# The first products of the RWKV solve ahead of the SSD's norm: a move on one NeuronCore

## The chip, the core and the metric

The program runs on one core of one Trainium2 chip. Its time is the device time in microseconds (us) of one execution, and the number that counts is the median of several runs. The core's engines run side by side, each works through its own list in order, and they wait for each other through semaphores: PE (TensorE, matrix products into PSUM banks), DVE (VectorE), ACT (ScalarE), POOL (GpSimd) and SP (SyncE, which only issues the weights' DMAs here). PE's clock has two levels, 1.2 and 2.4 GHz; the profile shows which was granted.

## What is computed, cut to what matters

Two transformer blocks follow each other on 256 tokens of width 1024. The first block mixes with an SSD (a chunked state-space mixer) and with RWKV-7, side by side:

```python
y = _ssd_chunked(xh, dt, A, Bm, Cm) + d_skip[:, None] * xh        # SSD, two chunks of 128 tokens
y = y.reshape(b, T, SSD_D) * silu(z)                              # gated
y = y.reshape(b, T, SSD_GROUPS, SSD_D // SSD_GROUPS)
y = y * rsqrt(mean(y * y, axis=-1, keepdims=True) + NORM_EPS)     # norm over each of two groups
y_ssd = y.reshape(b, T, SSD_D) * norm_g
...
def step(S, inp):                                                 # RWKV-7, one token
    r_t, w_t, k_t, v_t, a_t, b_t = inp
    sa = einsum("bhij,bhj->bhi", S, a_t)
    S = S * w_t[:, :, None, :] + sa[..., None] * b_t[:, :, None, :] + v_t[..., None] * k_t[:, :, None, :]
    return S, einsum("bhij,bhj->bhi", S, r_t)
...
mix = concatenate([y_ssd, y_rwkv], axis=-1) @ w_out               # then norm, feed-forward, second block
```

The second block attends to a memory of 256 rows; its keys, `rms_norm(mem) @ w_xk_2`, depend on nothing of the first block.

## The kernel before

**Layout.** Everything is held with the feature on the 128 partitions. Weights come in chunks through a ring of four slots (`ring`), loaded by SP in one fixed order; SP waits until the chunk four places earlier has been used. Intermediate values lie in one large tile, `arena`, by hand-written addresses; PSUM's eight banks are `banks[0]` to `banks[7]`. Nothing is scheduled by a planner: each engine's list is the order in which the functions are called at the file's end, and `mark` and `at` give a step a name and a semaphore value to wait for.

**The stretch in question** lies between the SSD and the first chunk of the RWKV solve.

- `pe_ssd` ends with the products of the SSD's outputs ("ssd y", L1010 and L1013). DVE (`dve_ssd`) adds the skip (L1086) and multiplies with the gate (L1090, "ssd gated"), then takes the reciprocal of the memory norm's root (L569, "mem rstd").
- The SSD's norm has these pieces. ACT squares the gated values (L1121); PE sums them over the partitions into columns of bank 0 (`pe_ssd_norm`, L1140); ACT takes the root (L1124); DVE the reciprocal of 4 columns (L1095, "ssd group rates"); PE spreads it over a bank (`pe_ssd_rates`, L1149, "ssd rates bank"); DVE writes the four normed tiles (L1098, "mix1" 0 to 3). Between them `column_rstd` (L576) turns the memory norm's rate into a column.
- The solve inverts a triangular matrix per head and chunk of 128 tokens, eight heads as two sets `g` of four. For each chunk `c`, `products` (L1514) and `base_products` (L1526) make the matrix L in banks 0 and 3 and its 32-wide blocks in banks 1 and 4; DVE masks them into `LT` and `X` (L1711 to L1719) and transposes `X` to `XT` (L1722). Then four levels follow, blocks of 2, 4, 8 and 16 doubling. In each PE makes "P bank" (L1573) from `LT` and `X`, DVE masks it to `P` (L1730), PE makes "dX bank" (L1584) from `XT` and `P`, and DVE adds it to `X` and transposes again (L1737, L1740). PE cannot go on without DVE, so `fill(n)` puts other products between: parts of the memory keys (`pe_mem_part`, L1252, 12 products of 128x256 in f16; two parts make a quarter of the weights' columns), the sums of RWKV's bonus (L1868) and of its gate (L1877), or products that only keep the clock (L1537).
- For the memory keys ACT writes the high half of each quarter of the weights (`mem_high`, L1224) and DVE the low half (`mem_low`, L1231); part 2n waits for `mem_low` n.
- POOL multiplies `R` and `KP` for the bonus (L1903, 128x1024) and clears two buffers of each set (L1842, L1843).

**What sets the order.** The level buffers of the solve (`solve_set`) lie from `SOLVE` on, where the SSD keeps `rawx`, `xbc`, `EX`, `MT` and `zs`; the two sets are 3584 columns each, all laid out alike. So PE, before chunk 0, waits for `mix1` 3 (L1098), the last reader of the SSD's place and of bank 1. POOL's L1903 and the clearing wait for `mix1` 3 too.

Of the kernel before, what the change touches and what calls it, by code (L numbers as in the profile page):

```python
# [23 lines left out]
P = 128  # L24
# [273 lines left out]
def build(nc, w, out, known):  # L298

    with ExitStack() as ctx:  # L300
# [85 lines left out]
        def solve_set(i):  # L386

            a = SOLVE + 3584 * i
            return dict(LT=view(a, 4, C), X=view(a + 512, 4, BASE), XT=view(a + 640, 4, BASE),
                        P=[view(a + 768, 4, BASE // 2), view(a + 832, 4, BASE // 2)], P32=view(a + 896, 4, BASE),  # L390
                        XT128=view(a + 1024, 4, C), X64=view(a + 1536, 4, 64), RK=view(a + 1792, 4, C),
                        ARB=view(a + 2304, 4, C), G=view(a + 2816, 4, 64), U=view(a + 3072, 4, 64))
# [624 lines left out]
        def dve_ssd(dve):  # L1017
# [63 lines left out]

            for g in range(2):
                dve.wait_ge(*at("ssd y", 1, g))
                for j in range(2):
                    i = 2 * g + j
                    nc.vector.scalar_tensor_tensor(YS[:, i, :], XS(i), par("ssd_d", i), halves(5 + g)[:, j, :],  # L1086
                                                   ALU.mult, ALU.add).then_inc(*mark("ssd_vector"))
                dve.wait_ge(*so_far("ssd_vector"))
                dve.wait_ge(*at("z silu", g))
                nc.vector.tensor_tensor(YS[:, 2 * g:2 * g + 2, :], YS[:, 2 * g:2 * g + 2, :],  # L1090
                                        zs[:, 2 * g:2 * g + 2, :], ALU.mult).then_inc(
                    *mark("ssd_vector", "ssd gated", g))
            norm_reciprocal(dve, "mem")
            dve.wait_ge(*at("ssd group root"))
            nc.vector.reciprocal(group_rate, group_rate).then_inc(*mark("ssd_vector", "ssd group rates"))  # L1095
            dve.wait_ge(*at("ssd rates bank"))
            for i in range(4):
                nc.vector.scalar_tensor_tensor(mix[:, i, :], YS[:, i, :], par("ssd_norm", i), halves(1)[:, i // 2, :],  # L1098
                                               ALU.mult, ALU.mult).then_inc(*mark("ssd_vector", "mix1", i))

        def act_ssd(act):
# [22 lines left out]
            nc.scalar.activation(group_rate, banks[0][:, 0:4], ACT.Sqrt, bias=eps[:, 0:1],  # L1124
# [9 lines left out]
        def pe_ssd_norm(pe):  # L1134
            for g in range(2):
                pe.wait_ge(*at("ssd squares", g))
                pe.wait_ge(*at("ssd exponent", 0, 1, 3))
                for c in range(NC_):
                    for j in range(2):
                        mm = nc.tensor.matmul(banks[0][:, 2 * g + c:2 * g + c + 1],  # L1140
# [4 lines left out]
        def pe_ssd_rates(pe):  # L1145
            pe.wait_ge(*at("ssd group rates"))
            pe.wait_ge(*at("k token-major"))
            for n in range(4):
                mm = nc.tensor.matmul(quarters(1)[:, n, :], group_rate[:, n:n + 1].broadcast_to([P, P]), ident,  # L1149
                                      start=True, stop=True)  # L1150
# [388 lines left out]
        def pe_rwkv_chunk(pe, c):  # L1539
# [14 lines left out]
            if c == 0:  # L1554
                pe.wait_ge(*at("k token-major"))
                pe.wait_ge(*at("AT"))
                pe.wait_ge(*at("mix1", 3))
# [6 lines left out]
            fill(0)  # L1564
            half = BASE // 2
            for n, m in enumerate(LEVELS):
                for g in range(2):
# [8 lines left out]
                    mm.then_inc(*mark("solve_pe", "P bank", c, g, n))  # L1576
                fill(1 + 2 * n)
# [126 lines left out]
        def dve_rwkv_chunk(dve, c):  # L1704
# [18 lines left out]
            if c == 0:  # L1723
                mem_low(dve, 1)
            for n, m in enumerate(LEVELS):
                half = BASE // 2
                mask = const("levels")[:, half * n:half * n + half]
                for g in range(2):
# [3 lines left out]
                                            over(mask, 4), ALU.mult).then_inc(*mark("solve_vector", "P", c, g, n))  # L1732
                for g in range(2):
# [10 lines left out]
                if n in (1, 3):  # L1744
                    mem_low(dve, 4 * c + n // 2 + 2)
# [91 lines left out]
        def pool_rwkv_chunk(pool, c):  # L1837

            if c == 0:
                pool.wait_ge(*at("mix1", 3))  # L1840
# [24 lines left out]
        def pe_bonus_sums(pe, i):  # L1865

            pe.wait_ge(*at("bonus products"))
            nc.tensor.matmul(banks[2 + 3 * i][:, :], head_ones, flat(A_)[:, 512 * i:512 * i + 512], start=True,  # L1868
# [29 lines left out]
        def pool_bonus(pool):  # L1898
# [3 lines left out]
            pool.wait_ge(*at("mix1", 3))  # L1902
# [911 lines left out]
        def _(pe):  # L2814
# [3 lines left out]
            pe_ssd_norm(pe)  # L2818
            column_rstd(pe, "mem", 7, ("mem", "root"))
            pe_ssd_rates(pe)  # L2820
# [171 lines left out]
```

## Time and profile before

| | us |
|---|---|
| median of 3 runs | 814.72 (811.87, 814.72, 814.74) |
| the profiled execution | 818.56, of which the span (first to last instruction) is 816.7 |
| PE busy | 785.5, 96% of the span |
| DVE busy | 540.2, 66% |
| ACT busy | 399.4, 49% |
| POOL busy | 77.3, 9% |
| DMA | 127.93 MB, 157 GB/s on average |
| chain that ended last, by engine | PE 72%, DVE 16%, ACT 6%, DMA 2%, issue 2% |

Busy times of different engines overlap and don't add up to the span. PE is busy nearly all the time, so a change is read from where PE is idle, and from where its instructions take longer than the same ones elsewhere. All times of rows are in us from the span's start.

### The profile page before, as it was taken

To read this page: it belongs to the slowest core of one execution; us is meant where nothing else is said; L and a number is where in the kernel's file an instruction comes from. 1 tells how busy PE (TensorE), PEld (TensorE's weight loads), DVE (VectorE), ACT (ScalarE), POOL (GpSimd) and SP (SyncE) were. 2 spreads that over 40 slices of the span, in tenths; PEclk is the share of its full clock that TensorE was granted. 3 is DMA by queue.
4 is the path that set the end of the run, shared out by engine and by line. 5 is a ranking of instruction groups with operands and counts; after the bars stand their busy time and mean duration, and the time that the engine had idled before them with its cause. 6 is when DMAs were issued, how large, how long until landed. Compare 5 with 4: busy or idle time off the path is not lost.

```text
span 816.7 us, 17184 instructions
## 1 busy us (share of the span) xinstructions
PE 785.5 (96%) x7486; PEld 664.6 (81%) x7486; DVE 540.2 (66%) x861; ACT 399.4 (49%) x639; POOL 77.3 (9%) x102
## 2 busy tenths in 40 slices
PE   7999978989999999999999999999999999999996
PEld 6788876777886888888886777688878888888885
DVE  4679765656358899999677886753575586664443
ACT  5458443121245666666554763162554475553333
POOL 1142111303002011111001000000200200000000
PEclk9999996999999999999999999999999999999998
DMA  9971230303038356555782463202828055556001
GB/s 333 383 277 75 104 116 2 107 2 107 3 104 308 106 204 207 207 207 194 271 303 110 151 257 110 99 6 104 307 107 301 10 191 196 195 215 228 9 1 52
DMA packets 66555, 127.93 MB, mean 157 GB/s; under 512 B 3760, under 2 KB 27568, under 8 KB 66352
## 3 DMA queue, kind: packets, MB, share of 16 engines
q1 hardware_dynamic: 65168, 122.92, 41.7%
q0 software_dynamic: 592, 2.69, 0.9%
q8 instruction: 59, 0.97, 0.5%
q10 hardware_dynamic: 720, 1.23, 0.4%
q14 instruction: 16, 0.13, 0.0%
HBM read 125.78 MB, written 1.05 MB: 155 GB/s over the span
## 4 chain that ended last, share of the span: by engine, by line
PE 72%; DVE 16%; ACT 6%; DMA 2%; issue 2%; SPq 1%; POOL 0%; DVEq 0%
PE bank L505 21%; PE bank L614 19%; DVE arena L493 8%; PE bank L611 7%; DVE arena L2073 3%; PE bank L2160 3%; PE bank L1252 3%; DMA ring<-in_w_in_dram 2%; ACT arena L484 2%; PE bank L762 2%; PE bank L737 2%; PE bank L1271 1%; PE bank L1514 1%; PE bank L2354 1%; SPq L450 1%
## 5 line engine op out<-in xcount | busy, mean ns | idle before, releaser
L493 DVE SCALAR_TENSOR_TENSOR arena<-ring,arena 128x1024 f16<-128x1024 f32 x194 | 230.2, 1233 | 78.8 <-ACT arena L484 78.4
L505 PE MATMUL bank<-hg,arena 128*128 128x256 f16 x2496 | 275.9, 273 | 1.0 <-DVE arena L493 1.0
L505 PEld LDWEIGHTS bank<-hg,arena 128*128 128x128 f16 x2496 | 243.0, 98 | 33.4 <-issue 3.5
L484 ACT ACTIVATE arena<-ring 128x1024 f16<-128x1024 f32 x194 | 191.9, 1045 | 91.3 <-PE bank L614 51.5
L614 PE MATMUL bank<-arena 128*128 128x256 f16 x1296 | 142.2, 273 | 0.2 <-DVE arena L493 0.2
L614 PEld LDWEIGHTS bank<-arena 128*128 128x128 f16 x1296 | 126.6, 98 | 15.5 <-issue 0.9
L611 PE MATMUL bank<-mix,ring 128*128 128x256 f32 x256 | 56.0, 379 | 0.0
L611 PEld LDWEIGHTS bank<-mix,ring 128*128 128x128 f32 x256 | 48.3, 190 | 6.6 <-issue 0.2
L520 ACT ACTIVATE hg<-h,params 128x256 f16<-128x256 f32 (+1 forms) x40 | 20.0, 499 | 57.3 <-DVE h L2568 43.7
L2073 DVE SCALAR_TENSOR_TENSOR arena<-arena,params 128x256 f32<-128x256 f32 x88 | 36.7, 480 | 0.7 <-ACT arena L2107 0.7
L505 PE MATMUL bank<-xv,arena 128*128 128x256 f16 x288 | 32.1, 273 | 0.0
L505 PEld LDWEIGHTS bank<-xv,arena 128*128 128x128 f16 x288 | 28.0, 98 | 3.9 <-issue 0.4
L2568 DVE SCALAR_TENSOR_TENSOR h<-bank,h 128x512 f32<-128x512 f32 x12 | 8.2, 687 | 33.4 <-PE bank L614 20.7
L538 POOL COPY ssum<-sqs 128x512 f32<-128x512 f32 x4 | 2.5, 614 | 255.8 <-ACT sqs L524 255.8
L569 DVE RECIPROCAL rstd<-rms 128x256 f32<-128x256 f32 x8 | 14.0, 1750 | 17.0 <-ACT rms L564 17.0
L2131 POOL TENSOR_TENSOR arena<-arena 128x256 f16<-128x256 f32 x22 | 14.3, 671 | 112.1 <-ACT arena L2121 112.1
L2160 PE MATMUL bank<-arena,hg 128*128 128x512 f16 x96 | 23.3, 401 | 0.1
L614 PE MATMUL bank<-mix,arena 128*128 128x256 f16 x192 | 21.1, 273 | 1.8 <-DVE mix L2676 1.8
L2121 ACT ACTIVATE arena<-arena 128x256 f16<-128x256 f32 x22 | 8.9, 417 | 27.9 <-DVE arena L2083 27.9
L2107 ACT ACTIVATE arena<-arena,params 128x256 f32<-128x256 f32 x44 | 19.8, 497 | 5.3 <-DVE arena L2064 5.3
L614 PEld LDWEIGHTS bank<-mix,arena 128*128 128x128 f16 x192 | 18.7, 98 | 4.3 <-DVE mix L2676 2.1
L2709 DVE SCALAR_TENSOR_TENSOR arena<-bank,rstd 128x512 f32<-128x512 f32 x16 | 11.0, 690 | 16.3 <-PE bank L505 16.2
(376 smaller groups left out, 969.1 us busy)
## 6 DMA issues: line engine op xcount, KB each, us to landing
ring<-in_w_in_dram SPq DMA_DIRECT2D x12, 2048.0 KB, 9.0
ring<-in_ffn_w_up_dram SPq DMA_DIRECT2D x22, 1024.0 KB, 7.3
ring<-in_w_ff_dram SPq DMA_DIRECT2D x8, 2048.0 KB, 9.0
ring<-in_w_ff_dram SPq DMA_DIRECT2D x16, 1024.0 KB, 6.3
ring<-in_ffn_w_down_dram SPq DMA_DIRECT2D x11, 1024.0 KB, 5.8
ring<-in_w_out_dram SPq DMA_DIRECT2D x8, 1024.0 KB, 6.3
ring<-in_w_xk_dram SPq DMA_DIRECT2D x2, 2048.0 KB, 10.4
ring<-in_w_xv_dram SPq DMA_DIRECT2D x2, 2048.0 KB, 8.1
```

Source lines behind the costliest of these rows:

```text
L484: nc.scalar.activation(quarter(halves_of(chunk)[0], chunk, q), quarter(slot(*chunk), chunk, q), ACT.Copy, scale=W_SCALE).then_inc(*mark("w ...
L493: nc.vector.scalar_tensor_tensor(quarter(halves_of(chunk)[1], chunk, q), quarter(slot(*chunk), chunk, q), W_SCALE, quarter(halves_of(chunk ...
L505: mm = nc.tensor.matmul(out_, weight[a][:, k, cols], src[:, k, b, :], start=(first and i == 0), stop=(last and i == 2), skip_group_check=True)
L520: nc.scalar.activation(hg16[:, m, 0, :] if split else hg[:, m, :], src[:, m, :], ACT.Copy, scale=par(gain, m)).then_inc(*mark("norm_gained ...
L611: return nc.tensor.matmul(out_, slot(name, "rows", i)[:, kk, cols], src[:, k, :], start=first, stop=last, skip_group_check=True)
L614: mm = nc.tensor.matmul(out_, halves_of((name, "rows", i))[a][:, kk, cols], src[:, k, b, :], start=(first and n == 0), stop=(last and n == ...
L737: mm = nc.tensor.matmul(halves(b % 4)[:, i % 2, :], slot("w_in", "z")[:, k, j * P:(j + 1) * P], hg[:, k, :], start=(k == 0), stop=(k == KT ...
L762: mm = nc.tensor.matmul(halves(b % 4)[:, i % 2, :], slot("w_in", kind)[:, k, j * P:(j + 1) * P], hg[:, k, :], start=(k == 0), stop=(k == K ...
L1252: mm = nc.tensor.matmul(halves(b)[:, n % 2, :], w_[:, a, k, :], mem16[:, k, x, :], start=(k == 0 and i == 0), stop=(k == KT - 1 and i == 2))
L2073: nc.vector.scalar_tensor_tensor(uacc[r][:, i, :], uraw[r][:, i, tap:tap + T], par("ffn_conv_w", 2 * FFT * tap + tile0 + i), uacc[r][:, i, :],
L2107: nc.scalar.activation(uacc[r][:, i, :], uraw[r][:, i, 2:T + 2], ACT.Copy, scale=par("ffn_conv_w", 2 * 2 * FFT + 2 * p + FFT * (b % 2) + i ...
L2160: mm = nc.tensor.matmul(banks[bank][:, :], hg16[:, k, b, c * C:(c + 1) * C], w_[a][:, k, :], start=(k == 0 and n == 0), stop=(k == KT - 1 ...
```

## The change

The buffers of the solve that are written in its first steps (`LT`, `X`, `XT`, `P`) get addresses outside the SSD's place. PE makes chunk 0's `products` and `base_products` right behind "ssd y". The SSD's sums and the memory column follow them, level 0's "P bank" comes next, then the rates' bank (now bank 5 in place of bank 1; the sums are now in bank 2 in place of bank 0). DVE takes the memory reciprocal ahead of the skip and gate, the 4-column reciprocal behind the first masks, and the four normed tiles behind level 0. `mem_low` 1 moves into level 1, `mem_low` 2 behind level 2. POOL's waits for `mix1` 3 become waits for "ssd mt" 1 1 and "ssd gated" 1, and the first sum of the bonus waits for `mix1` 3. Shortened:

```diff
         def solve_set(i):
             a = SOLVE + 3584 * i
-            return dict(LT=view(a, 4, C), X=view(a + 512, 4, BASE), XT=view(a + 640, 4, BASE),
-                        P=[view(a + 768, 4, BASE // 2), view(a + 832, 4, BASE // 2)], P32=...,
-                        ... RK=view(a + 1792, 4, C),
+            lt, rk, x, xt, p = ((SOLVE + 7424, a + 1792, SOLVE + 7936, 4624, 4752),
+                                (a + 1792, a, a + 3328, a + 3456, a + 2688))[i]
+            return dict(LT=view(lt, 4, C), X=view(x, 4, BASE), XT=view(xt, 4, BASE),
+                        P=[view(p, 4, BASE // 2), view(p + 64, 4, BASE // 2)], P32=...,
+                        ... RK=view(rk, 4, C),
...
+            norm_reciprocal(dve, "mem")
             for g in range(2):
                 dve.wait_ge(*at("ssd y", 1, g))
...
-            norm_reciprocal(dve, "mem")
+        def dve_ssd_rates(dve):
             dve.wait_ge(*at("ssd group root"))
...
+        def dve_ssd_end(dve):
             dve.wait_ge(*at("ssd rates bank"))
...
             if c == 0:
                 pe.wait_ge(*at("k token-major"))
                 pe.wait_ge(*at("AT"))
-                pe.wait_ge(*at("mix1", 3))
...
             products(c, 0, BT, AT_, "LT bank")
             base_products(c)
-            fill(0)
+            if c == 0:
+                pe_ssd_norm(pe)
+                column_rstd(pe, "mem", 7, ("mem", "root"))
+            else:
+                fill(0)
...
+                if c == 0 and n == 0:
+                    pe_ssd_rates(pe)
+                    fill(0)
                 fill(1 + 2 * n)
...
             if c == 0:
-                mem_low(dve, 1)
+                dve_ssd_rates(dve)
...
+                if c == 0 and n == 1:
+                    mem_low(dve, 1)
                 for g in range(2):
                     st = sets[g]
                     grown = even(flat(st["X"]), m)
...
+                if c == 0 and n == 0:
+                    dve_ssd_end(dve)
-                if n in (1, 3):
-                    mem_low(dve, 4 * c + n // 2 + 2)
+                if n in (2 - c, 3):
+                    mem_low(dve, 4 * c + (3 if n == 3 else 2))
...
         def pool_rwkv_chunk(pool, c):
             if c == 0:
-                pool.wait_ge(*at("mix1", 3))
+                pool.wait_ge(*at("ssd gated", 1))
...
         def pe_bonus_sums(pe, i):
             pe.wait_ge(*at("bonus products"))
+            pe.wait_ge(*at("mix1", 3))
...
         def pool_bonus(pool):
-            pool.wait_ge(*at("mix1", 3))
+            pool.wait_ge(*at("ssd mt", 1, 1))
...
             pe_ssd(pe)
-            pe_ssd_norm(pe)
-            column_rstd(pe, "mem", 7, ("mem", "root"))
-            pe_ssd_rates(pe)
             for c in range(NC_):
                 pe_rwkv_chunk(pe, c)
```

The order of PE's list, from the last product of the SSD's outputs to the first level of the solve. Line numbers are those of each kernel: L1514, L1526, L1573 and L1584 of before are L1520, L1532, L1582 and L1596 of after; L1140, L576, L1149 and L1252 are L1146, L578, L1155 and L1258. Before:

```order
L1013 MATMUL bank<-mix,xv 64x128
L1140 MATMUL bank<-consts,arena 128x1 x8
L576 MATMUL bank<-consts,rstd 128x1 x2
L1149 MATMUL bank<-consts,small 128x128 x4
L1514 MATMUL bank<-arena 128x128 x8
L1526 MATMUL bank<-arena 32x32 x32
L1252 MATMUL bank<-xk,sqs 128x256 x12
L1573 MATMUL bank<-arena 32x16 x32
L1537 MATMUL bank<-consts 128x512 x2
L1584 MATMUL bank<-arena 32x16 x32
```

After:

```order
L1015 MATMUL bank<-mix,xv 64x128
L1520 MATMUL bank<-arena 128x128 x8
L1532 MATMUL bank<-arena 32x32 x32
L1146 MATMUL bank<-consts,arena 128x1 x8
L578 MATMUL bank<-consts,rstd 128x1 x2
L1582 MATMUL bank<-arena 32x16 x32
L1155 MATMUL bank<-consts,small 128x128 x4
L1258 MATMUL bank<-xk,sqs 128x256 x12
L1543 MATMUL bank<-consts 128x512 x2
L1596 MATMUL bank<-arena 32x16 x32
```

The first two products of the solve moved from behind the three norm pieces to ahead of them, and the rates' bank moved behind level 0's "P bank".

The order of DVE's list from level 0 to level 1; L1730, L1737, L1740 and L1231 of before are L1742, L1751, L1754 and L1237 of after, and L1104 (before L1098) writes the normed tiles. Before:

```order
L1231 SCALAR_TENSOR_TENSOR mix<-ring,mix 128x1024
L1730 TENSOR_TENSOR arena<-bank,consts 128x64 x2
L1737 TENSOR_TENSOR arena<-bank,arena 128x32x2
L1740 STREAM_TRANSPOSE arena<-arena 128x128
L1737 TENSOR_TENSOR arena<-bank,arena 128x32x2
L1740 STREAM_TRANSPOSE arena<-arena 128x128
L1730 TENSOR_TENSOR arena<-bank,consts 128x64 x2
L1737 TENSOR_TENSOR arena<-bank,arena 128x16x4
```

After:

```order
L1099 RECIPROCAL small<-small 128x4
L1742 TENSOR_TENSOR arena<-bank,consts 128x64 x2
L1751 TENSOR_TENSOR arena<-bank,arena 128x32x2
L1754 STREAM_TRANSPOSE arena<-arena 128x128
L1751 TENSOR_TENSOR arena<-bank,arena 128x32x2
L1754 STREAM_TRANSPOSE arena<-arena 128x128
L1104 SCALAR_TENSOR_TENSOR mix<-mix,params,bank 128x256 x4
L1742 TENSOR_TENSOR arena<-bank,consts 128x64 x2
L1237 SCALAR_TENSOR_TENSOR mix<-ring,mix 128x1024
L1751 TENSOR_TENSOR arena<-bank,arena 128x16x4
```

The four normed tiles now stand between level 0 and level 1, and `mem_low` 1 moved from ahead of level 0 into level 1, behind its mask.

## Rows read from the trace of the kernel before

**Rows 1.** Page, part 2: PE's granted clock in 40 slices, in tenths.

```profile
PEclk9999996999999999999999999999999999999998
```

**Rows 2.** Chain that ended last, in order of time: start, us, engine and line.

```profile
127.21 0.85 PE bank L576 x4
128.06 1.93 PE bank L1149 x8
130.01 1.67 DVE mix L1098 x4
...
160.14 1.09 PE bank L1514 x16
```

**Rows 3.** PE in order of time: start, us, count, idle before in brackets.

```profile
119.76 0.45 PE L1010 MATMUL bank<-arena,xv 128*64 128x128 f32 x4 [4.18 <-DVE arena L1079]
...
122.14 0.75 PE L1013 MATMUL bank<-mix,xv 128*64 128x128 f32 x4
123.63 3.58 PE L1140 MATMUL bank<-consts,arena 128*128 128x1 f32 x16 [0.74 <-ACT arena L1121]
...
131.81 2.08 PE L1514 MATMUL bank<-arena 64*128 64x128 f32 x16 [1.84 <-DVE mix L1098]
133.82 0.89 PE L1526 MATMUL bank<-arena 64*32 64x32 f32 x64
134.64 2.74 PE L1252 MATMUL bank<-xk,sqs 128*128 128x256 f16 x12
137.32 0.81 PE L1573 MATMUL bank<-arena 32*32 32x16 f32 x64
138.06 0.60 PE L1537 MATMUL bank<-consts 128*128 128x512 f16 x2
138.60 0.73 PE L1584 MATMUL bank<-arena 32*32 32x16 f32 x64
139.25 1.48 PE L1252 MATMUL bank<-xk,sqs 128*128 128x256 f16 x12
...
141.32 1.12 PE L1868 MATMUL bank<-arena,consts 128*128 128x512 f32 x2
...
150.44 0.30 PE L1573 MATMUL bank<-arena 32*32 32x16 f32 x12 [1.30 <-issue]
```

**Rows 4.** DVE in order of time, same columns.

```profile
119.03 1.28 DVE L1079 TENSOR_TENSOR arena<-arena 128x512 f32<-128x512 f32 x2
121.22 0.87 DVE L1086 SCALAR_TENSOR_TENSOR mix<-arena,params,bank 128x256 f32<-128x256 f32 x2 [0.91 <-PE bank L1013]
...
124.44 1.74 DVE L569 RECIPROCAL rstd<-rms 128x256 f32<-128x256 f32 x1
...
133.97 0.69 DVE L1711 TENSOR_TENSOR arena<-bank,consts 128x512 f32<-128x512 f32 x1 [2.30 <-PE bank L1514]
...
136.83 0.31 DVE L1722 STREAM_TRANSPOSE arena<-arena 128x128 f32<-128x128 f32 x1
137.06 1.18 DVE L1231 SCALAR_TENSOR_TENSOR mix<-ring,mix 128x1024 f16<-128x1024 f32 x1
...
139.83 0.31 DVE L1740 STREAM_TRANSPOSE arena<-arena 128x128 f32<-128x128 f32 x1
```

**Rows 5.** Stretches: length, busy of PE, PEld, DVE, ACT, POOL, then PEclk, DMA.

```profile
120.00:121.00 1.00, 1.00 (x18) 1.00 (x16) 0.31 (x1) 0.99 (x2) 0.00 (x0) 0.75 0.07 16
126.00:130.00 4.00, 3.98 (x18) 3.68 (x18) 0.36 (x2) 1.38 (x3) 0.00 (x0) 0.50 0.00 0
...
137.00:138.00 1.00, 1.00 (x66) 0.69 (x64) 1.00 (x2) 0.00 (x0) 0.00 (x0) 0.72 0.00 0
```

**Rows 6.** POOL in order of time.

```profile
131.85 2.34 POOL L1903 TENSOR_TENSOR arena<-arena 128x1024 f32<-128x1024 f32 x1 [14.06 <-DVE mix L1098]
```

**Rows 7.** ACT in order of time.

```profile
124.56 0.63 ACT L1121 ACTIVATE arena<-mix 128x512 f32<-128x512 f32 x1 [0.98 <-DVE mix L1090]
```

**Rows 8.** Waits over the whole span: us in total, times, longest.

```profile
ACT arena L484 <- DMA ring<-in_w_in_dram: 6.1, 2, 5.0
```

More of the change, by code:

```diff
@@ L388, in solve_set @@
             a = SOLVE + 3584 * i
-            return dict(LT=view(a, 4, C), X=view(a + 512, 4, BASE), XT=view(a + 640, 4, BASE),
-                        P=[view(a + 768, 4, BASE // 2), view(a + 832, 4, BASE // 2)], P32=view(a + 896, 4, BASE),
-                        XT128=view(a + 1024, 4, C), X64=view(a + 1536, 4, 64), RK=view(a + 1792, 4, C),
+            lt, rk, x, xt, p = ((SOLVE + 7424, a + 1792, SOLVE + 7936, 4624, 4752),
+                                (a + 1792, a, a + 3328, a + 3456, a + 2688))[i]
+            return dict(LT=view(lt, 4, C), X=view(x, 4, BASE), XT=view(xt, 4, BASE),
+                        P=[view(p, 4, BASE // 2), view(p + 64, 4, BASE // 2)], P32=view(a + 896, 4, BASE),
+                        XT128=view(a + 1024, 4, C), X64=view(a + 1536, 4, 64), RK=view(rk, 4, C),
                         ARB=view(a + 2304, 4, C), G=view(a + 2816, 4, 64), U=view(a + 3072, 4, 64))
@@ L1092, in dve_ssd @@
                     *mark("ssd_vector", "ssd gated", g))
-            norm_reciprocal(dve, "mem")
+        def dve_ssd_rates(dve):
             dve.wait_ge(*at("ssd group root"))
             nc.vector.reciprocal(group_rate, group_rate).then_inc(*mark("ssd_vector", "ssd group rates"))
+        def dve_ssd_end(dve):
             dve.wait_ge(*at("ssd rates bank"))
             for i in range(4):
-                nc.vector.scalar_tensor_tensor(mix[:, i, :], YS[:, i, :], par("ssd_norm", i), halves(1)[:, i // 2, :],
+                nc.vector.scalar_tensor_tensor(mix[:, i, :], YS[:, i, :], par("ssd_norm", i), halves(5)[:, i // 2, :],
                                                ALU.mult, ALU.mult).then_inc(*mark("ssd_vector", "mix1", i))
@@ L1123, in act_ssd @@
             act.wait_ge(*at("ssd group total"))
-            nc.scalar.activation(group_rate, banks[0][:, 0:4], ACT.Sqrt, bias=eps[:, 0:1],
+            nc.scalar.activation(group_rate, banks[2][:, 0:4], ACT.Sqrt, bias=eps[:, 0:1],
                                  scale=1.0 / 256).then_inc(*mark("ssd_act", "ssd group root"))
@@ L1139, in pe_ssd_norm @@
                     for j in range(2):
-                        mm = nc.tensor.matmul(banks[0][:, 2 * g + c:2 * g + c + 1],
+                        mm = nc.tensor.matmul(banks[2][:, 2 * g + c:2 * g + c + 1],
                                               xbc[:, 2 * g + j, c * C:(c + 1) * C], ones[:, 0:1],
@@ L1148, in pe_ssd_rates @@
             for n in range(4):
-                mm = nc.tensor.matmul(quarters(1)[:, n, :], group_rate[:, n:n + 1].broadcast_to([P, P]), ident,
+                mm = nc.tensor.matmul(quarters(5)[:, n, :], group_rate[:, n:n + 1].broadcast_to([P, P]), ident,
                                       start=True, stop=True)
```

## The prediction

> **What bounds the kernel now.** I read the page's clock row first [rows 1]: 40 slices, and but for the seventh (122 to 143 us) PE's clock is nearly whole; there it is 0.6. The change works in that slice. The chain that ended last runs through it [rows 2]: PE's L1140, L576 and L1149, then DVE's L1098, then PE's L1514. PE in order of time [rows 3] gives what can be had. The last product of the SSD's outputs ends at 122.14 + 0.75 = 122.89. PE then waits 0.74 for the squares, and 1.84 (from 129.98 to 131.81) for the four normed tiles. These 2.58 us are all of its idle time between 122.89 and the end of level 0's L1584, at 138.60 + 0.73 = 139.33. The third term is the clock. It fell between 120 and 121, behind 4.18 us without work [rows 3, 5], and rose between 137 and 138. All work between runs at the lower of the two levels, 1.2 GHz: the same 16 products of L1514 take 2.08 here and 1.09 at 160 us [rows 2, 3], and the 12 of L1252 take 2.74 against 1.48 [rows 3].
>
> **The change, part by part.** The sum is made from 122.89 on, with PE in its new order. No work is added or taken away but for waits.
>
> Step 1, the order up to level 0's L1584, first with the clock low as long as before. L1514 needs inputs that were ready long ago, so it runs 122.89 to 124.97 and L1526 to about 125.8 (0.89, of which the next overlaps the last 0.07). Then L1140. Its squares come a little later than now, since DVE takes the 1.74 us reciprocal L569 first [rows 4]: 0.91 of it fills the idle time ahead of L1086, 0.83 pushes the gate back. The second gate is done at 124.44 + 0.83, about 125.3, its squares 0.63 later [rows 7], near 126.0. The first squares are there at 124.4. So L1140 starts at 125.8 and doesn't wait: 3.58 to 129.4, L576 0.85 to 130.2, L1573 0.81 to 131.0, L1149 1.93 to 132.9, part 0 of the memory keys (L1252) 2.7 to 135.6. L1537 took 0.54 at full clock (138.06 to 138.60) and would take twice that, to 136.7; L1584 0.65 (138.60 to 139.25), to 137.35. Before this was 139.33: 2.0 us gained, the 2.58 of idle less 0.54 for L1537.
>
> Step 2, what hides the rest. DVE's first masks go from 133.97 to 137.14 in before, 3.17 us for both sets [rows 4]. They can start at 125.3, so `X` is ready at 128.5; PE asks for it at 130.2: 1.7 us of cover. The root and the small reciprocal follow L1140's end at 129.4 and are due at L1149, 131.0. In before they fit beside L576's 0.85, since L1149 followed without a wait: at least 0.7 of cover. POOL's product (2.34) [rows 6] starts at 120.3 in place of 131.85 and is due only behind ACT's `mem_high` 1, after 131. If PE ran at full clock from 124 on, the first cover would be gone: PE would stand at `X` until 128.5. That bounds the gain from above (below).
>
> Step 3, the new wait. The normed tiles (1.67 us) now stand between DVE's level 0 and level 1, and PE's first bonus sum, L1868, waits for them; behind it on PE stand L1584 of level 1 and all that follows. DVE ends level 0 0.81 us behind the end of L1584 (139.83 + 0.31 against 139.33), and the tiles 1.67 later: 2.48. PE is there after part 1 and L1573, 141.32 - 139.25 = 2.07 [rows 3]. So PE waits 0.4, with the semaphore 0.45. The mask of level 1 (in level 0 it fits beside L1537's 0.54) and `mem_low` 1 (1.18) follow on DVE: ready 4.1 to 4.2 us behind L1584, due at 2.52 + 1.06 (L1868 less its overlap) + 0.65 = 4.2. This is just hidden; each 0.1 more costs 0.1. `mem_low` 2, one level later, is due two fills later and is hidden by more than 2 us. Steps 1 and 3 together: 2.0 - 0.45 = 1.6 us gained at least.
>
> Step 4, the clock. The trace has no row of this order, so I bound it. At worst the clock rises no earlier than now: nothing. In before it rose behind L1514, L1526 and L1252 in one run, 131.81 to 137.3. In the new order there are two such runs: 119.76 to 125.8 (the outputs' products, L1514, L1526), and from 131.0 on (L1149, L1252). If the second does it, at about 134, half of L1252's extra 1.3 and L1537's 0.54 come back, 1.2 us. If the first does it, L1514's second half and L1526 run at double speed, 0.7 more, and part of L1140 too. If it rises there and stays, PE meets `X` at 128.5, then L1573 0.7, L1149 1.0, L1252 1.42, L1537 0.54, L1584 0.66: 132.8, a gain of 6.5, less the tiles' wait 6.0. I take 1.5, near the row of the run that did raise it: 131 is 0.8 earlier than 131.81 and the first run is a second chance. From 126 to 130 PE worked 3.98 of 4 us, on L1140, L576 and L1149, and the clock stood at 0.50 [rows 5], so I don't count on its staying whole while L1140 and L576 run.
>
> The Trainium skill, page "TensorE: Matmul & The Clock Gate", section "HAM oscillation — how this bites in real kernels", says that PE's clock drops on long idle gaps and that work packed without gaps keeps it. By it the order after, with no gap from 119.8 on, should recover and stay, near the upper bound of 6.0. The row of 126 to 130, busy and still slow, speaks against so much.
>
> Step 5, the rest of the program. Behind 143 us the lists are the same, and all engines there hang on PE or on each other. No load paces them: ACT's two waits for a chunk of `w_in` [rows 8], the first weights of the program, are the only long ones of a compute engine for the ring's loads on the way, and a load waits for the last user of its slot, which moves along. So what is gained at level 1 should arrive at the end. One thing can change: there are stalls that nothing in the profile explains, the longest 1.30 us within L1573 at 149 [rows 3], and the clock may dip near them. They may change by their own length either way.
>
> Sum: 816.7 - 1.6 - 1.5 = 813.6 for the span, 815.5 for the profiled execution (818.56). That execution is 3.8 us longer than the median of the runs shown; the same 3.1 us off the median of 814.72 give 811.6.
>
> **The rivals.** (a) The clock comes back in the first run and stays: a gain of 6.0, 808.7. For it: six microseconds without a gap. Against: the 4.4 us of L1140 and L576 stand right behind, and they lie wholly in the low stretch of before.
> (b) The clock gives nothing, or DVE's start is late: a gain of 1.6, 813.1. One mechanism would be POOL's 2.34 us product and DVE's L569 side by side from 120.3. If they excluded each other, L569 would run 122.7 to 124.4, the squares would come at 126.8 and 128.3, and L1140 would start 1.0 later: 3.1 - 1.0 = 2.1 gained, 812.6. For it: both now start within 0.1 us; in before POOL's product met no DVE work. Against: L569 reads one operand of SBUF.
> The Trainium skill, page "SBUF — State Buffer", section "SBUF: two separate sides", says DVE and GpSimd lock a shared port for a whole instruction, when DVE reads two SBUF inputs or runs in a two-port mode. By it L1079 and L1090 collide with the product and L569 need not; no run here shows it yet.
> (c) The gain is given back in the levels. There PE ran 17 us from 131.81 on and then met the 1.30 us stall; an engine that runs on sooner can meet it sooner and longer. A stall of twice the length (1.3 more), and one more stretch at half clock (1.8 for 3.6 us of it), take the 3.1: no change, 814.7.
> (d) Slower: the clock stays low through the levels. what stood ahead of the rise in before was L1514, L1526 and L1252, 5.5 us; the last run ahead of the levels is now L1149 and L1252, 4.6 us. If it rises at level 3 only, near 149, three L1252 cost 1.26 each more, two L1868 1.1 each, L1573 and L1584 some 0.1 to 0.3 each: 6.5 us, less the 1.6 gained, is 4.9 slower, 819.6. It decides against the change from a rise later than about 141.
>
> **How the numbers follow.** Forecast, 2.2 to 4.0 gained: 0.50. (a) 0.13, (b) 0.18, (c) 0.13, (d) 0.06. The predicted time is the forecast's, 811.6. The range goes from 808.2, below (a), to 815.2, above (b) and above (c) by half a microsecond; what lies outside is (d), a tail of (c), and (a) together with a run like the 811.87 of before, some 0.15 in all. A difference of 0.5% is 4.07 us, about what a measurement of this kernel can tell from none. Faster by more: (a) and a quarter of the forecast, 0.13 + 0.13, 0.26. Slower by more: 0.05, most of (d). Within: 0.69.
>
> **What would show it.** Right: PE's row of L1520 (the old L1514) starts within 0.1 us of the outputs' end; no idle of over 0.2 until the first L1885 (the old L1868), and there 0.3 to 0.9 behind DVE's L1104; L1582 of level 0 doesn't wait for the transposes unless the clock is whole; the clock is whole before 137. From level 1 on all rows stand 2 to 4 us earlier, up to the end. Wrong in step 2: PE waits for L1734. Wrong in step 3: a wait of over 1 us for L1104, or L1258 waiting for L1237. Wrong in step 4: L1258's first part takes 2.7 whole. Wrong in step 5: the gain at level 1 is larger than at the end.

## The result, and the profile after

| | before | after | ratio |
|---|---|---|---|
| first comparison, median | 814.47 us | 806.66 us (806.24 to 807.78, 4 executions) | 0.991, 95% interval 0.989 to 0.993 |
| repeated (`after_again`) | 814.37 | 808.80 (806.57 to 809.56, 6) | 0.993 (0.992 to 0.994) |
| repeated (`after_same`) | 814.06 | 808.89 (807.09 to 811.72, 6) | 0.9945 (0.993 to 0.996) |

The change makes the kernel faster by 7.8 us in the first comparison and by 5.6 and 5.2 in the repeats. All 16 executions of after together have a median of 808.0, so I take the gain for about 6. The forecast was 3.1 (811.6, range from 808.2). The first comparison and the median of all 16 lie below the range, the two repeats just inside it.

The profiled execution of after took 806.24 us, its span 804.4, the fastest of the 16. The profile of before took 818.56, 4 us above its median. So the two pages differ by 12.3 us, twice what the medians show, and sizes below come from several traces of each order.

The functions are the same with new line numbers: L1514 is L1520, L1526 is L1532, L1140 is L1146, L576 is L578, L1573 is L1582, L1149 is L1155, L1252 is L1258, L1537 is L1543, L1584 is L1596, L1868 is L1885, L1098 is L1104, L1722 is L1734.

The page's clock row of after, against [rows 1]:

```profile
PEclk9999999999999999999999999999999999999998
```

The slice with 0.6 is gone. PE of after in order of time, the answer to [rows 3]:

```profile
119.27 0.70 PE L1012 MATMUL bank<-arena,xv 128*64 128x128 f32 x4 [4.18 <-DVE arena L1081]
...
122.62 1.16 PE L1520 MATMUL bank<-arena 64*128 64x128 f32 x16
123.71 0.76 PE L1532 MATMUL bank<-arena 64*32 64x32 f32 x64
124.40 1.95 PE L1146 MATMUL bank<-consts,arena 128*128 128x1 f32 x16
126.20 0.59 PE L578 MATMUL bank<-consts,rstd 128*128 128x1 f32 x4
126.72 0.44 PE L1582 MATMUL bank<-arena 32*32 32x16 f32 x32
127.41 0.44 PE L1582 MATMUL bank<-arena 32*32 32x16 f32 x32 [0.25 <-DVE arena L1734]
127.78 1.16 PE L1155 MATMUL bank<-consts,small 128*128 128x128 f32 x8
...
133.84 1.10 PE L1885 MATMUL bank<-arena,consts 128*128 128x512 f32 x2 [0.43 <-DVE mix L1104]
```

L1520 starts without idle behind the outputs' products and takes 1.16 us where L1514 took 2.08. L1146 takes 1.95, L1140 took 3.58. Two small waits are left, 0.25 for the transposes and 0.43 for the normed tiles. The stretches of [rows 5] in after (length, busy of PE, PEld, DVE, ACT, POOL, then PEclk, DMA):

```profile
120.00:121.00 1.00, 1.00 (x12) 1.00 (x9) 1.00 (x1) 1.00 (x2) 1.00 (x1) 0.50 0.00 0
126.00:130.00 4.00, 3.75 (x92) 3.47 (x92) 1.68 (x7) 2.97 (x7) 0.00 (x0) 1.00 0.01 4
137.00:138.00 1.00, 1.00 (x66) 0.93 (x66) 0.45 (x2) 0.00 (x0) 0.00 (x0) 1.00 0.00 0
```

From 126 to 130 the clock is whole (1.00); in before it was 0.50 there. The chain that ended last, in order of time, has changed engines, against [rows 2]:

```profile
119.81 1.55 DVE rstd L571
...
124.36 0.68 DVE arena L1723
...
127.05 0.32 DVE arena L1734
...
127.41 0.44 PE bank L1582 x32
127.85 1.09 PE bank L1155 x8
```

Where it ran over PE's slow L1140, L576 and L1149, it now runs over DVE's list, from the reciprocal L571 to the last transpose. DVE sets the pace of after up to 127.4 in this execution, so a still faster PE would gain nothing there.

DVE's reciprocal and POOL's product, which the prediction feared would exclude each other:

```profile
119.73 1.75 DVE L571 RECIPROCAL rstd<-rms 128x256 f32<-128x256 f32 x1
119.99 2.36 POOL L1920 TENSOR_TENSOR arena<-arena 128x1024 f32<-128x1024 f32 x1 [2.70 <-DVE arena L1081]
```

They run side by side, and each takes within 0.02 us as long as alone (1.74 and 2.34 in [rows 4, 6]). The Trainium skill, page "SBUF — State Buffer", section "SBUF: two separate sides", lets them run together, since L571 reads one operand of SBUF; the trace agrees.

### The profile page after: what moved, and what is told of

Same layout as the page of the kernel before. It is cut to its first block, busy times and chain, and to the rows that moved or that the text cites. A ratio compares the mean times of both kernels' runs of the same rounds, so it can differ in the third digit from the quotient of the medians.

```text
span 804.4 us, 17186 instructions
## 1 busy us (share of the span) xinstructions
PE 776.5 (97%) x7486; PEld 658.8 (82%) x7486; DVE 540.2 (67%) x861; ACT 399.5 (50%) x639; POOL 77.4 (10%) x102
## 4 chain that ended last, share of the span: by engine, by line
PE 71%; DVE 18%; ACT 5%; DMA 2%; issue 2%; SPq 1%; POOL 0%; DVEq 0%
PE bank L507 22%; PE bank L616 19%; DVE arena L495 8%; PE bank L613 7%; DVE arena L2090 3%; PE bank L2177 3%; PE bank L1258 2%; DMA ring<-in_w_in_dram 2%; ACT arena L486 2%; PE bank L764 2%; PE bank L739 2%; PE bank L1277 1%; PE bank L2639 1%; PE bank L2371 1%; PE bank L1520 1%
## 5 line engine op out<-in xcount | busy, mean ns | idle before, releaser
L571 DVE RECIPROCAL rstd<-rms 128x256 f32<-128x256 f32 x8 | 14.0, 1750 | 16.3 <-ACT rms L566 16.3
L2726 DVE SCALAR_TENSOR_TENSOR arena<-bank,rstd 128x512 f32<-128x512 f32 x16 | 11.0, 690 | 16.3 <-PE bank L507 16.2
L2177 PE MATMUL bank<-arena,hg 128*128 128x512 f16 x96 | 21.6, 380 | 0.1
```

What stands on the lines that cost most here:

```text
L2177: mm = nc.tensor.matmul(banks[bank][:, :], hg16[:, k, b, c * C:(c + 1) * C], w_[a][:, k, :], start=(k == 0 and n == 0), stop=(k == KT - 1 ...
```

## The experiments

**The question.** The idle time removed accounts for 2.1 us of a gain of about 6. My theory is that the rest is the clock: PE runs from the outputs' products straight into the solve's, the clock comes back at 122 to 126 us in place of 138 to 139, and less work runs at half speed. The rivals: that only waits count, and the clock would be paid back in later waits; and that the gain lies elsewhere, in the stall at 149.

Each kernel ran beside before on the same chip. Ratios are to before. In the summary, "waits" is PE's idle time for other engines from the end of the outputs' products to level 2, "low" the time between 117 and 140 us with the clock at the lower level, and "to level 2" the distance from the first of the outputs' products behind the wait of 4.18 us to level 2's memory part, all from the profiled execution.

| kernel | waits | low | L1140 or L1146 | to level 2 | median | ratio |
|---|---|---|---|---|---|---|
| before | 2.6 | 17.1 | 3.58 | 23.3 | 814.5 | |
| before_again | 2.5 | 20.5 | 3.57 | 24.0 | 814.10 | 1.000 |
| before_keep | 4.1 | 10.2 | 2.84 | 22.4 | 812.98 | 0.9985 |
| before_dense | 1.9 | 10.2 | 2.09 | 21.8 | 813.21 | 0.9989 |
| before_hold | 1.3 | 6.8 | 2.19 | 22.6 | 811.09 | 0.9959 |
| before_shift | 3.1 | 13.7 | 2.10 | 22.7 | 815.11 | 1.001 |
| after | 0.7 | 3.4 | 1.95 | 16.3 | 806.66 | 0.991 |
| after_again | 0.4 | 10.3 | 1.95 | 18.3 | 808.80 | 0.993 |
| after_same | 0.4 | 10.3 | 1.95 | 19.2 | 808.89 | 0.9945 |
| after_mix | 0 | 10.3 | 1.95 | 18.0 | 809.61 | 0.995 |
| after_gap | 1.3 | 6.8 | 1.95 | 18.5 | 808.84 | 0.9935 |
| after_keep | 1.5 | 6.8 | 2.10 | 18.9 | 808.70 | 0.9931 |
| after_gap_long | 2.9 | 20.5 | 3.57 | 24.2 | 814.53 | 1.000 |
| after_late | 3.1 | 20.5 | 3.55 | 24.3 | 815.20 | 1.002 |

**before_again, before unchanged.**

> The kernel before, unchanged, run again to see how its low-clock stretches differ from run to run. The trace of before has 27 us at the low clock behind the start (120.5 to 137.6, and 3.4 us each at 151.2, 181.9 and 513.0) and its run took 818.56, 4 us over the median. Theory 1 (the gain is the clock's: the low stretch from 120 us on lasts 17 us in before and 3.4 in after): the runs of before are long where their mean clock is low, and none has a clock of 0.990 or more; median 814.5. Theory 2 (the gain is the 2.6 us of idle and a chance difference in the clock): some runs of before reach the 0.992 of after and then take about 809.

Measured: 814.10, ratio 1.000 (0.999 to 1.001), over 12 executions. This is the spread against which the others are read.

**after_again and after_same, after unchanged,** in two later comparisons.

> The changed kernel, unaltered, beside the others of this job. Expected: 806.7, ratio 0.991 to before, and mean granted clocks of 0.989 to 0.994 over its executions, against 0.979 to 0.988 for before. If the first four executions of after were a lucky draw of the clock, it lies at 808 to 810.

> The changed kernel unaltered again, beside the three others of this job, since it measured 806.7 in its first four executions and 808.8 in the next six. Expected 808.0 to 808.8, a gain of 5.5 to 6.5. If the first ones were right, 806.7.

Measured: 808.80 and 808.89. The 806.66 of the first comparison, four executions, lies at the low end of what after takes: a lucky draw, as the first expectation allowed. PE of `after_again` in order of time:

```profile
124.07 1.82 PE L1520 MATMUL bank<-arena 64*128 64x128 f32 x16
125.81 0.76 PE L1532 MATMUL bank<-arena 64*32 64x32 f32 x64
126.50 1.95 PE L1146 MATMUL bank<-consts,arena 128*128 128x1 f32 x16
128.31 0.58 PE L578 MATMUL bank<-consts,rstd 128*128 128x1 f32 x4
128.82 1.04 PE L1582 MATMUL bank<-arena 32*32 32x16 f32 x64
129.79 2.08 PE L1155 MATMUL bank<-consts,small 128*128 128x128 f32 x8
131.66 1.79 PE L1258 MATMUL bank<-xk,sqs 128*128 128x256 f16 x12
```

The clock comes back within L1520 and is whole for L1146 and L578. It falls again at 128.9, as L1582 begins, though PE had no idle time from 120.40 on, and L1155 and a part of L1258 run at the lower level. In the first profile of after this second low stretch is missing. To level 2 `after_again` takes 2 us more than that profile; a part of that is the clock's earlier return in `after` (122.2 against 125.5), the rest this stretch.

**after_gap and after_gap_long, a wait ahead of the solve's products.** The first waits for the first gate's squares, the second (`0` made `1`) for both.

```diff
             if c == 0:
                 pe.wait_ge(*at("k token-major"))
                 pe.wait_ge(*at("AT"))
+                pe.wait_ge(*at("ssd squares", 0))
```

> The kernel after, with one more wait: PE's first products of the solve wait for the first squares of the SSD's norm, ready 0.9 us behind the end of the SSD's output products (123.6 against 122.7 in the trace of after). It splits the unbroken run of PE in two. Theory 1: the clock comes back later in many runs, 2 to 5 us slower than after, 808.7 to 811.7, with a low stretch of 6.8 us or more from 119 on. Theory 2: only the wait counts, and DVE needs the products 0.4 us later than they come now: 0.4 slower, 807.1.

> After, but PE waits for both squares before the solve's first products: a gap of about 1.6 us, as long as the waits of after_late up to the norm sums, with only the order of the two pieces of work behind it differing. Theory A (the order decides: behind the gap the products of 64x128 and 64x32 columns first, then the sums of one column; the clock comes back as in after): 1.6 to 2 over after_same, 809.6 to 810.8, and a low stretch of under 8 us. Theory B (the unbroken run decides, and the gap breaks it): the clock stays low past L1146 as in after_late, 812.5 to 815.

Measured: 808.84 (0.9915 to 0.9955) with the gap of 0.85 us, as fast as the repeats of after (the low stretch is the 6.8 us of theory 1, but not the loss of 2 us or more); 814.53 (0.999 to 1.0015) with the long gap, as slow as before. PE of `after_gap_long`:

```profile
122.84 0.69 PE L1015 MATMUL bank<-mix,xv 128*64 128x128 f32 x4
125.98 2.08 PE L1520 MATMUL bank<-arena 64*128 64x128 f32 x16 [2.44 <-ACT arena L1127]
127.99 0.89 PE L1532 MATMUL bank<-arena 64*32 64x32 f32 x64
128.81 3.57 PE L1146 MATMUL bank<-consts,arena 128*128 128x1 f32 x16
132.24 0.99 PE L578 MATMUL bank<-consts,rstd 128*128 128x1 f32 x4
```

The gap is 2.44 us, and the kernel loses 5.6 against `after_same`. L1146 takes 3.57 again, and the clock stays low to 138.6. Order, buffers and all other waits are those of after. So the order alone brings nothing: what pays is that the solve's products stand close behind the outputs' products. Theory B, that a gap of this length loses the gain, holds by the medians (12 executions against the 6 of `after_same`); the gap of 0.85 us cost nothing that can be told. A single profile says less. In `after` the granted clock was whole from 122.2 on, before L1520 began at 122.62, and in `after_gap` from 123.4, within the gap: there only the outputs' products stood ahead of its return.

**after_late, the norm's sums back ahead of the solve's products,** all else as in after.

```diff
+            if c == 0:
+                pe_ssd_norm(pe)
+                column_rstd(pe, "mem", 7, ("mem", "root"))
             products(c, 0, BT, AT_, "LT bank")
             base_products(c)
-            if c == 0:
-                pe_ssd_norm(pe)
-                column_rstd(pe, "mem", 7, ("mem", "root"))
-            else:
+            if c:
                 fill(0)
```

> After, with the SSD's squared sums and the column sum (L1146, L578) put back ahead of the solve's first products, so that PE again waits for the squares behind the outputs' products; all else as in after. Theory 1 (the gain is mostly the clock, which comes back because PE runs from the outputs' products straight into the solve's first products): the wait of about 1.6 us returns and the clock stays low through those products, 4 us more: 811.5 to 813. Theory 2 (only waits count): 1.6 us over after, 808.3, with a low stretch of under 8 us.

Measured: 815.20, ratio 1.002 (1.0004 to 1.003), 6.4 us slower than `after_again` beside it and a little slower than before; 2 us above what theory 1 gave. PE of `after_late`:

```profile
124.25 3.55 PE L1146 MATMUL bank<-consts,arena 128*128 128x1 f32 x16 [0.85 <-ACT arena L1127]
127.65 0.99 PE L578 MATMUL bank<-consts,rstd 128*128 128x1 f32 x4
128.58 2.08 PE L1520 MATMUL bank<-arena 64*128 64x128 f32 x16
130.58 0.89 PE L1532 MATMUL bank<-arena 64*32 64x32 f32 x64
132.51 0.62 PE L1582 MATMUL bank<-arena 32*32 32x16 f32 x32 [1.04 <-DVE arena L1734]
133.96 0.62 PE L1582 MATMUL bank<-arena 32*32 32x16 f32 x32 [0.82 <-DVE arena L1734]
```

With the sums first the gap is only 0.85, but the clock doesn't come back, and the masks then come so late that PE waits 1.04 and 0.82 for them, which I had not priced. So three other parts of the change (the rates behind level 0's "P bank", the tiles between the levels, POOL's early product) show no gain without this one. By the medians the gain needs both: no long gap, and the products of 64x128 and 64x32 ahead of those of one column. It is not so that before's order can't have the clock back: `before_dense` and `before_shift` below had it whole from 122.3 and 122.8 on, behind the outputs' products alone, and then lost it again. The clock fell at another moment in every profile (between 117.5 and 120.5 where nothing filled the wait of 4.18 us), and what this does to its return isn't separated here from what the order does.

**before_keep and after_keep, products that nobody reads in the wait of 4.18 us.**

```diff
             for c in range(NC_):
+                if c == 1:
+                    pe.wait_ge(*at("k token-major"))
+                    pe_keep_clock(14)
```

> The kernel before, with 14 products of 128x512 in f16 (0.22 us each at full clock, 3.0 in all) in PE's 4.18 us wait ahead of the last SSD products (119.76 us). They write to a bank that nobody reads. Theory 1: the clock doesn't fall at 120.5; by the same products at full clock the end of level 0 comes 4.8 us earlier than 139.3, unless the 1.84 us wait for the normed tiles lets the clock fall there; median 809 to 811.5. Theory 2: 814.2 to 814.8, no change.

> The kernel after, with the same 14 products in the same wait. Theory 1: no low stretch at 118.8 to 122.2 (3.4 us in the trace of after). DVE's chain (reciprocal, gate, masks, from 119.7 to 127.4) doesn't shorten with it, since DVE didn't wait for PE there but 0.1 us, so the gain is small: 0 to 0.7, 806.0 to 806.7, and steadier. Theory 2: 806.7, no change.

Measured: 812.98 (0.997 to 1.000) and 808.70 (0.992 to 0.994). In both the outputs' products run at full clock. In before PE then waits 1.85 us for the squares where it waited 0.74, and the clock falls at 125.2 behind that wait. In after the squares make PE wait 0.56 and 0.46, and the clock falls at 126.5. The low stretch is moved, not removed. In before 1.1 us comes of it, between the two theories (809 to 811.5, and no change); in after nothing, and the 806.0 to 806.7 expected of `after_keep` was missed by 2, as its reference was the lucky first comparison.

**before_hold, such products in all three waits of before** (14, then 7 behind `pe_ssd`, then 7 ahead of the wait for `mix1` 3).

> Before, with products of 128x512 that nobody reads in all three of PE's waits: 14 in the one of 4.18 us, 7 behind the outputs' products, 7 ahead of the wait for the normed tiles. The order and the waits of before stay, only the clock should be kept. Theory 1 (the clock from 120 to 138 is worth 4 to 5 us): 809 to 810, low stretch under 7 us in the profile. Theory 2 (a whole clock only lengthens the waits for DVE and ACT, since these pace PE there): 812.5 to 814.

Measured: 811.09, ratio 0.9959 (0.995 to 0.997), a gain of 3.3 with before's order and before's waits. PE of `before_hold`:

```profile
121.72 1.69 PE L1540 MATMUL bank<-consts 128*128 128x512 f16 x7
123.64 2.19 PE L1143 MATMUL bank<-consts,arena 128*128 128x1 f32 x16 [0.23 <-ACT arena L1124]
125.78 1.01 PE L576 MATMUL bank<-consts,rstd 128*128 128x1 f32 x4
126.65 2.06 PE L1152 MATMUL bank<-consts,small 128*128 128x128 f32 x8
128.50 3.19 PE L1540 MATMUL bank<-consts 128*128 128x512 f16 x7
131.62 1.63 PE L1517 MATMUL bank<-arena 64*128 64x128 f32 x16
```

The two waits are still paid, and more, as work nobody needs: the last 7 products take 3.19 at the lower clock, the wait in their place was 1.84. So holding the clock is worth some 3 us to the kernel in before's order, less than theory 1's 4 to 5. The six executions stand in the order of their mean clock: 809.09 us at 0.998, 810.20 at 0.996, 810.63 at 0.994, 811.54 and 812.07 at 0.991, 813.04 at 0.990. The profiled one is the last. It comes to level 2 only 0.7 to 1.4 us sooner than the two profiles of before, and its stall in the levels was short (0.14), so how the 3.3 divide between this stretch and the rest isn't shown. In the order of before a fast PE meets DVE and ACT sooner and waits for them.

**before_dense, only the 7 behind `pe_ssd`.**

> Before, with 7 products of 128x512 that nobody reads behind the SSD's outputs' products and nothing in the wait of 4.18 us. They take 3.0 us at half clock, 0.65 to 1.3 of it beside a wait that is there anyway. Theory A (wide products right behind the outputs' products bring the clock back, whatever they are): the clock rises at about 125 and L1143, L576 and perhaps L1152 run whole, so the 2 us that the products cost come back: 812.5 to 814.5, and a low stretch of 3.4 to 7 us. Theory B (the clock needs something else of the change): it stays low until about 138, and the time is 815.5 to 816.5.

Measured: 813.21, ratio 0.9989 (0.998 to 1.000). PE of `before_dense`:

```profile
122.70 1.68 PE L1537 MATMUL bank<-consts 128*128 128x512 f16 x7
124.22 2.09 PE L1140 MATMUL bank<-consts,arena 128*128 128x1 f32 x16
126.27 0.61 PE L576 MATMUL bank<-consts,rstd 128*128 128x1 f32 x4
126.89 1.16 PE L1149 MATMUL bank<-consts,small 128*128 128x128 f32 x8
129.88 2.08 PE L1514 MATMUL bank<-arena 64*128 64x128 f32 x16 [1.84 <-DVE mix L1098]
```

L1140, L576 and L1149 take 3.9 us in place of 6.6, and the time lies in theory A's range. But the filling products did not bring the clock back, as theory A has it. It was whole from 122.3 on, 0.4 us before the first of them, as the mean of this stretch shows (length, busy of each engine, PEclk, DMA):

```profile
122.00:123.00 1.00, 1.00 (x13) 0.71 (x11) 0.97 (x3) 0.55 (x1) 0.00 (x0) 0.86 0.00 0
```

What the trace shows of them is that the clock stayed whole over them and the three pieces behind. Then the wait of 1.84 stays, the clock falls again within it, at 129.1, L1514 runs at 2.08, and the low stretches sum to 10.2 us where theory A had 3.4 to 7. The change has products that have to be made anyway in that place, and no such wait behind them.

**after_mix, the wait for the normed tiles only where it is needed.**

```diff
-            pe.wait_ge(*at("mix1", 3))
+            if i:
+                pe.wait_ge(*at("mix1", 3))
```

> After, with the wait for the normed tiles only ahead of the second bonus sum, not of the first, which does not write the bank that the tiles' rates are read from. The wait of 0.43 us ahead of L1885 in level 1 should go. If PE sets the pace there: 0.4 below after_same. If DVE's level 1 mask then comes late (it is ready only just in time in the working of the prediction): PE waits up to 0.4 us for it one group later, and nothing is gained.

Measured: 809.61 (ratio 0.995, 0.994 to 0.996), beside 808.89 for `after_same`. The wait of 0.43 is gone from the trace, and level 2 comes after 18.0 us where it is 18.3 in `after_again`, with low stretches of the same length. The median shows nothing of it. The executions of after spread over 5 us, so 0.4 can't be told here. No version that I ran beats after.

**before_shift, all of PE's instructions 96 places later.** 48 products of one column at the program's start, where PE waits for the input.

```diff
             pe.wait_ge(*at("identity landed"))
+            for _ in range(48):
+                nc.tensor.matmul(banks[2][:, 0:1], ..., start=True, stop=True, skip_group_check=True)
```

> Before, with 48 products of 128x1 that nobody reads at the program's start, where PE waits for the input: nothing changes but the place of each later instruction in PE's stream, by 96. If the stall of 1.30 us in level 3 (and those like it) comes from the fetch of PE's instructions, it goes or moves, and the profile shows PE's levels without it; worth 1 to 3 us with the low clock behind it: 811 to 813. If it comes from the data or the clock, it stays at the same products and the time stays at 814.1.

Measured: 815.11, ratio 1.001 (1.000 to 1.002): the time stays, as the second theory has it, though not for its reason. The first row is PE of `before_again`, the second, in its own fence, of `before_shift`:

```profile
151.29 0.30 PE L1573 MATMUL bank<-arena 32*32 32x16 f32 x12 [1.30 <-issue]
```

```profile
150.31 1.49 PE L1255 MATMUL bank<-xk,sqs 128*128 128x256 f16 x12 [0.93 <-issue]
```

Counting all of PE's instructions in the trace from 0 (matmuls, weight loads and those of its sequencer), the stall of before ends at number 2754, that of `before_shift` at 3010, and those of `before_keep`, `before_dense` and `before_hold` at 2498. The remainder by 256 is 194 in all of them, and so it is for the stalls in chunk 1 of both orders, at 4290, 4546 and 4802 (one less in two of the traces). One of PE's instruction fetches (16 KB on its own DMA queue) landed 1.4 us ahead of the stall's end in both profiles of before (at 148.99 and 149.85, against 150.44 and 151.29). So the stall belongs to a place in PE's instruction stream, not to the data and not to the clock; that PE waits there for the fetch is inferred from the place and the landings. The shift moves it to the next such place and the time stays: that 1 to 3 us would go with it was wrong.

The Trainium skill, page "Runtime: NRT & Kernel Launch", section "Instruction fetch mechanics", has the fetch in blocks of 256 instructions, which these places agree with, and says that it is hidden behind the issue of instructions. If the stalls are the fetch's, it is not hidden in runs of products of 32x16: they last 0.1 to 1.3 us here.

The profile of `before_shift` also has the clock back behind the outputs' products, in before's order and with nothing in its waits:

```profile
123.00:126.00 3.00, 2.17 (x17) 2.05 (x18) 2.80 (x4) 0.78 (x3) 0.00 (x0) 1.00 0.00 0
```

It was whole from 122.8 to 126.2, and L1143 (L1140 of before) took 2.10 in two halves. But PE then waited 0.65 for each half and 1.84 for the tiles, the clock fell again, and level 2 came after 22.7 us, 0.6 and 1.3 sooner than in the two profiles of before and 3.5 to 4.4 later than in the repeats of after. A whole clock at L1140 alone bought little there.

## Why the prediction was too small

**Step 1, the order, was right.** L1520 follows the outputs' products without a wait, the 2.58 us of idle are gone, and L1146 doesn't wait for its squares.

**Step 2 was right.** In the first profile PE meets L1734 for 0.25 us, which the prediction allowed if the clock was whole, and in the repeats it doesn't.

**Step 3 was right to 0.02 us.** The new wait for the normed tiles is 0.43 or 0.44 (0.45 predicted) in every profile with this wait, and `mem_low` 1 is just hidden.

**Step 4 was the term that failed: 1.5 us taken, 2.4 to 5.3 measured.** I compare the rows from L1520 to the first L1258 with the same products in `before_again`. L1146 and L578 alone give 1.6 + 0.4 = 2.0 in `after_again` (1.95 and 0.58 for 3.57 and 0.99). I had put these outside the sum, because from 126 to 130 in before PE was 3.98 of 4 us busy on them with the clock at 0.50 [rows 5]. That row shows that such work doesn't raise the clock. It says nothing on whether the clock falls under it, and it doesn't at once: L1146 took 1.95 in the profiles of `after`, `after_again`, `after_same`, `after_mix` and `after_gap` alike. So the size was wrong because "I don't count on its staying whole while L1140 and L576 run" put at nothing what was worth 2.0. The first part of rival (a) came true in every profile of after. Its second part, that the clock stays, came true once in four (after); in `after_again`, `after_same` and `after_mix` it fell again behind L1146, at 126.8 to 128.9. The time of (a), 808.7, is near that of the repeats, in part by luck: the clock did not stay in them, to level 2 they gained 4.1 to 5.6 us on the two profiles of before and not 6.0, and the rest came behind level 2, where (a) has nothing. From the first of the outputs' products to the end of level 0's L1596 it is 12.1, 14.1 and 15.0 us in the three profiles of after, 19.6 and 20.3 in the two of before: 4.6 to 8.2 gained where 3.5 was forecast (2.0 and 1.5).

The rule of the Trainium skill, page "TensorE: Matmul & The Clock Gate", section "HAM oscillation — how this bites in real kernels", that long idle gaps cost the clock and gapless work keeps it, came nearer than my bound: the clock does come back behind a run without gaps. That such a run keeps it, the trace of `after_again` denies (low again from 128.9 to 132.3, without idle).

**Step 5 assumed nothing behind level 1, and something was there.** The stall in level 3 (or the level next to it) was 1.30, 1.30, 0.88, 0.99, 0.93 and 0.14 us in the six profiles of before's order, on average 0.92, and at most 0.53 in the eight of after's, `after_late` and `after_gap_long` among them, on average 0.12. In three of the six a low stretch of the clock began within 2 us behind it, in none of the eight: L1252 took 2.68 in `before_again` at 153.56 where 1.48 is its whole-clock time. In chunk 1 the stalls sum to 0.6 to 1.6 us in before's order and 0.3 to 2.6 in after's, with no difference on average. Rival (c) had the stall growing; it shrank. Why the order ahead of level 1 makes it shorter I can't say: the same instructions stand at the same places from there on. This is left open.

**The balance** of one pair, `before_again` and `after_again` (815.65 and 809.56, 6.1 apart): to level 2 5.6 us, of which 2.1 are waits and 3.5 the clock; 2.6 more to the memory part behind level 0 of chunk 1 (at 182.77 and 174.74), 1.1 of it the stall and the rest the low stretch behind it; 1.7 given back by longer stalls in chunk 1; 0.3 given back after. Sum 6.2 for 6.0 of the spans (813.8 and 807.8), the rest being where the first of the outputs' products stands.

How the 6 us divide beyond this pair isn't settled. The 15 executions of before with a mean clock of 0.988 average 813.8 us, the 3 of after with the same mean clock 809.1: 4.8 apart, more than the 2.1 of the waits. So the order also earns at the same clock, in part, it seems, because before's waits grow when its clock is back early (3.1 us in `before_shift`, 2.5 in `before_again`).

**Rivals (b) and (d)** fell: no delay on DVE beside POOL, and the clock came back at the first chance. But (d)'s mechanism is real. It stood one wait away: `after_late` and `after_gap_long` show the clock low up to 138 and no gain at all.

## What to carry to other kernels

When work is reordered behind a long wait, ask what stands in the first few microseconds behind it: with the wide products there the kernel was 6 us faster, with the same products behind a further wait of 2.4 us or behind sums of one column it was not faster at all. A clock that comes back is not yet a gain: in before's order it came back early too, in two profiles, and was lost again in or behind the waits. A row that shows work at half clock behind a gap doesn't say that this work lowers the clock; look for the same kind of work behind a run at full clock before pricing it. And take sizes from several profiles of each kernel, since single ones differed here by more than the term in question.

## What was not expected of the hardware

- A wait costs more than its length where it keeps the clock low: 2.44 us of wait cost 5.6 us of time (`after_gap_long` against `after_same`).
- The clock's return differs between executions of one order: in before's order it stayed low for 17.1 and 20.5 us in two profiles, and in a third (`before_shift`, 96 instructions at the start more) it was back after 3.4.
- The clock fell within a run with no idle time of PE (`after_again` at 128.9, behind L1146 and L578 with one column each), although not in every execution (not in `after`).
- PE stalls at most once in 256 of its instructions, always at the same place of the stream, by 0.1 to 1.3 us where it works through products of 32x16; 96 instructions more moved the place and not the time.
